# Three of layer 1's six modulation groups move from layer 0's choice of tokens to layer 1's output stage

## The reference, cut to what matters

```
sh1, sc1, g1, sh2, sc2, g2 = split((silu(c) @ ada_w + ada_b), 6)
csh1, csc1, cg1, csh2, csc2, cg2 = split(silu(c_ctx) @ ada_w + ada_b, 6)
hl = rmsnorm(xl, norm1_g) * (1 + sc1) + sh1
...
xl = xl + g1 * (concatenate([a_l, b_l, cv_l]) @ w_o)
xl = xl + g2 * ec_ffn(rmsnorm(xl, norm2_g) * (1 + sc2) + sh2, router_w, w_gate, w_up, w_down)
```

## Time and profile before

| | us |
|---|---|
| median of three runs | 4601.5 |
| lowest and highest | 4600.21 and 4602.4 |
| the profiled execution | 4604.36 |
| its span in the trace | 4602.6 |
| PE busy, of the span | 4057.6 (88%) |
| DVE busy | 2123.7 (46%) |
| ACT busy | 1224.3 (27%) |
| POOL busy | 731.9 (16%) |

### The profile page before, as it was taken

How to read it: one execution, slowest core, us unless ns; L and a number is a source line. 1 busy time by engine, 2 the same in 40 slices (tenths; PEclk the granted TensorE clock), 3 DMA queues, 4 the chain that set the end, 5 groups by cost and what they waited for, 6 DMA issues and landing times. The chain is left out here.

```text
span 4602.6 us, 76751 instructions
## 1 busy us (share of the span) xinstructions
PE 4057.6 (88%) x30527; PEld 2782.0 (60%) x30527; DVE 2123.7 (46%) x4242; ACT 1224.3 (27%) x2442; POOL 731.9 (16%) x858
## 2 busy tenths in 40 slices
PE   6998989987999799899986998999887988699994
PEld 4674557444888577566544886767566645465552
DVE  1213547226555422455425553121196767565554
ACT  1112336131000111244421000111165433133333
POOL 0110000311111011000111110000173042122222
PEclk8998999988999899999988999999899989799997
DMA  7115101348877611411129996311251312599995
GB/s 252 41 47 133 24 11 39 120 161 336 273 275 266 185 60 47 122 24 44 37 83 368 332 336 228 135 50 41 85 129 45 90 61 105 195 388 382 383 383 229
DMA packets 234733, 752.83 MB, mean 164 GB/s; under 512 B 62884, under 2 KB 139244, under 8 KB 216872
## 3 DMA queue, kind: packets, MB, share of 16 engines
q1 hardware_dynamic: 206664, 647.49, 39.5%
q0 software_dynamic: 21808, 73.42, 5.9%
q10 hardware_dynamic: 6000, 28.31, 1.6%
HBM read 650.48 MB, written 107.06 MB: 165 GB/s over the span
## 5 line engine op out<-in xcount | busy, mean ns | idle before, releaser
L3611 PE MATMUL bexp_gu<-up,bexp_xT 128*32 128x256 f32 x6144 | 342.0, 382 | 32.2 <-DMA up<-in_w_expert_up 18.2
L3611 PEld LDWEIGHTS bexp_gu<-up,bexp_xT 128*32 128x32 f32 x6144 | 209.1, 111 | 163.9 <-issue 33.2
L2059 PE MATMUL l0exp_gu<-l0exp_xT,l0e_held 128*128 128x160 f32 x2048 | 288.2, 302 | 4.5 <-DVE l0exp_xT L2103 4.5
L2059 PEld LDWEIGHTS l0exp_gu<-l0exp_xT,l0e_held 128*128 128x128 f32 x2048 | 280.7, 191 | 11.4 <-issue 6.2
L2059 PEld LDWEIGHTS l1exp_gu<-l1exp_xT,l1e_held 128*128 128x128 f32 x2048 | 233.8, 193 | 10.3 <-issue 7.2
L2059 PE MATMUL l1exp_gu<-l1exp_xT,l1e_held 128*128 128x128 f32 x2048 | 235.4, 276 | 2.7 <-DVE l1exp_xT L2103 2.7
L627 PE MATMUL p_ring<-p_hT,p_wc 128*128 128x256 f32 x1008 | 220.7, 382 | 4.8 <-DMA p_wc<-in_w_in 4.8
L3562 ACT ACTIVATE bexp_y<-bexp_acc,slot_gates 32x256 f32<-32x256 f32 x384 | 179.1, 467 | 148.2 <-PE bexp_acc L3596 139.2
L627 PEld LDWEIGHTS p_ring<-p_hT,p_wc 128*128 128x128 f32 x1008 | 192.5, 191 | 31.6 <-issue 5.1
L635 PE MATMUL p_ring<-p_wt,p_hT 128*128 128x400 f32 (+2 forms) x480 | 170.8, 516 | 0.0
L1119 PE MATMUL l0mla_scores<-l0mla_kT,l0mla_qT 96*128 96x512 f32 (+1 forms) x312 | 143.0, 546 | 21.1 <-DMA l0mla_qT<-RT 15.3
(11 more groups left out here) (700 smaller groups left out, 7756.9 us busy)
## 6 DMA issues: line engine op xcount, KB each, us to landing
up<-in_w_expert_up SPq DMA_DIRECT2D x31, 4096.0 KB, 23.8
l0e_held<-in_exp_w_gate SPq DMA_DIRECT2D x16, 2048.0 KB, 8.1
l0e_held<-in_exp_w_up SPq DMA_DIRECT2D x16, 2048.0 KB, 13.2
l0e_held<-in_exp_w_down SPq DMA_DIRECT2D x16, 2048.0 KB, 12.0
l1e_held<-in_exp_w_gate SPq DMA_DIRECT2D x16, 2048.0 KB, 8.4
l1e_held<-in_exp_w_up SPq DMA_DIRECT2D x16, 2048.0 KB, 12.9
l1e_held<-in_exp_w_down SPq DMA_DIRECT2D x16, 2048.0 KB, 13.3
near_space<-in_w_expert_down SPq DMA_DIRECT2D x16, 2048.0 KB, 24.3
```

The source lines that it names most:

```text
L2059: mm = nc.tensor.matmul(gu[g % 2][:, h, :], w[j][:, k, f * 128:(f + 1) * 128], xT[j][:, k, :], start=(k == 0), stop=(k == KD - 1))
L3611: mm = nc.tensor.matmul(gu[r][32 * c:32 * c + 32, 0:2 * HN].rearrange("p (h n) -> p h n", h=2), xT[j][:, k, 32 * r:32 * r + 32], both[:, : ...
```

## The change

Layer 0's choice of tokens makes groups 0 to 2 of layer 1. Layer 1's output stage makes groups 3 to 5, as layer 0's does for its own layer. Layer 1's choice still makes all six groups of the second block.

```
@@ -2185,7 +2185,7 @@
                             conv=(P1, Z, t["conv_w"][l], lambda tile: 1 if tile < CTX_TILES else 3),
-                            modulate=(lambda st: modulate(st, 0, [3, 4, 5], 1)) if l == 0 else None, energy=energy)
+                            modulate=lambda st: modulate(st, l, [3, 4, 5], 1), energy=energy)
@@ -2196,7 +2196,7 @@
                 route_choice(nc, n + "route", choices, X, a2, b2, t["router_w"][l], XN, energy, identity,
-                             lambda st: modulate(st, l + 1, list(range(6)), 3, expert.held), expert)
+                             lambda st: modulate(st, l + 1, list(range(3 if both else 6)), 3, expert.held), expert)
```

## The result

| | median us | runs | lowest and highest |
|---|---|---|---|
| before | 4602.4 | 9 | 4598.28 and 4613.57 |
| changed | 4618.5 | 9 | 4610.90 and 4628.58 |

The ratio is 1.0029, with a 95% interval of 1.0020 to 1.0037: 9 to 17 us slower, by the medians 16.1. The forecast was 4618.8 and +17.3. In a later series the changed kernel stood at 1.0027 (1.0017 to 1.0037). The profiled execution has a span of 4618.8 us, 16.2 over that of before.

The account below looks back on a forecast made before the run. It took DVE's search to bound layer 0's choice and PE layer 1's output stage. Blocks 16.72, clock 1.79, opening -1.21 and 0 elsewhere gave +17.3 us, a median of 4618.8 us, range 4614 to 4625.

Parts of the forecast that it names:

- The search sets layer 0's choice: Layer 0's choice of tokens: DVE's 36.84 us search sets the time, so removing groups 3 to 5 gains 0.
- about 27 us: Layer 0's choice: PE's idle time before the final transposes would grow from 7 to this, with DVE as releaser.
- 19.70 us: Layer 0's choice: how much earlier PE would be done without groups 3 to 5, 1068.99 in place of 1088.69.
- the rival of the time given back: Layer 0's choice: PE's chain of groups, not the search, releases the final transposes; sum -2.4 us, 4599.1 us; chance 4%.
- 1.43 us: End of layer 0's choice: possible gain from the barrier holding POOL, as the last gate store goes; kept as other end.
- The first expert's earlier loads: Layer 0's choice: SP issues the loads behind products 0 and 1, nobody waits for them; 0 both ways.
- The blocks: Layer 1's output stage: three added groups between tiles cost 6.61, 6.45 and 3.66 us, together 16.72 us.
- The clock: Behind the groups in layer 1's output stage: one fall of 1.69 us plus 0.10, 1.79 us; ends 0 and 5.07.
- The opening: Start of layer 1's output stage to its third tile: 1.21 us shorter with the load, as in layer 0.
- The end "+1": Opening of layer 1's output stage: other end, +1 us, with first convolutions late and the clock no better.
- The sum: Whole kernel: 16.72 + 1.79 - 1.21 + 0 = +17.3 us, median 4618.8 us, 0.38% slower.

Follow-up runs that it names:

- the removed half alone: Against the kernel before, layer 0's choice makes groups 0 to 2 only; nobody makes 3 to 5, layer 0's stand in: 0.9998, -1 us.
- e1: Against the kernel before, layer 0's choice keeps six groups and layer 1's output stage makes groups 3 to 5 once more: 1.0040, +18 us.
- e4: Against the kernel before, layer 1's choice makes both gates last and issues the first expert's loads ahead of the late stores: 0.9996, -2 us.
- e0: The changed kernel once more, against the kernel before: 1.0027, +12 us.
- e6: Kernel before with gates last in both choices, layer 0's choice products behind the last transpose of shares, late output-stage transposes in layer 0: 0.9992, -4 us.
- e10: Kernel with gates last and late transposes, one second-block gate moved from layer 1's choice to its output stage: 0.9977, -11 us against the kernel before.

## Why the prediction was right

- *The search sets layer 0's choice, and the removed groups are worth 0.* Shown: the removed half alone moved nothing (-6 to +3 us), PE's idle time grew to 32 us with DVE as its releaser, and the search kept its 36.8 us. The "about 27 us" of the forecast was a wrong reading, and with it the 19.70 us: PE was said to be done at 1068.99, but that is the end of group 3, one of those that leave. The last group that stays is group 2, in the order of time of the kernel before (a window of its own):

```profile
1057.33 6.23 PE L161 MATMUL l0route_modacc<-l0e_held,silu 128*2 128x256 f32 x64
```

It ends at 1063.56, 25.13 us ahead of 1088.69, and 25.13 + 6.97 is 32.10. The step was priced at 0, so the forecast did not suffer, but the rival of the time given back would have been worth 25.1 us and not 19.7. The prediction also overlooked that POOL's last row ended only 0.11 us before DVE's next step; where the two meet (e1, e4), the six groups cost up to 1.5 us, a gain for which it had no term (its 1.43 us were those of the barrier).

- *The first expert's earlier loads change nothing.* From the final transposes to the first expert transpose it is 7.29 us (before 7.22), and from there to the end of layer 0's experts as long as before.
- *The blocks.* 8.55, 8.38 and 5.38 us were forecast from layer 0 at 8.55, 8.39 and 5.38. The sum of 16.72 stands.
- *The clock.* One fall of 1.69 us and the 0.10 were taken, and that is what the profile has. That there was exactly one is in part luck. The reason for it, "once in two", was too coarse: in the old form of the block, in seven profiles of layer 0's stage and four of layer 1's, the records behind the first group were slow in 9 of 11, and those behind the second in 2 of 11. That is 11 falls in 11 stages, one for each on the average, as taken; single stages had none, one or two. The Trainium skill (TensorE: Matmul & The Clock Gate, "What's actually happening") says that activity releases the half rate. With the transposes late, the same two-row products stood alone between the tiles, with no idle time behind them, and in 16 blocks of eight stages the clock never fell behind them. So the traces fit the rule only through what else the old block had, the 1.70 us of waiting and the eight small transposes behind it. The edit moved both at once, and which of them it was no run shows.
- *The opening.* The step was right in its sign and too small: -1.21 was taken, -2.07 came. The 34.80 repeats (34.85, 34.87 and 34.81 in three others with three groups and the first 48 products at full clock; 35.91 with the gate 5 alone), and without a load it is 36.3 to 36.9. Layer 0, from which the term was taken, has 34.8 to 35.9. The end "+1" was not wide enough: where the first 48 products took 22.56 us in place of 20.87, four stages with and without a load took 38.7 to 39.1 us.
- *The sum.* The stage grew by 16.53 where 17.3 was forecast, the difference being the opening. The span's 16.2 is close to this in part by luck, as said above. The median moved by 16.1; the ratio's interval, 9 to 17 us, holds the 16.1 and ends just below 17.3, and in the series of e0 it is 8 to 17 us around 12.
- *The rivals.* The one on the other side (the chain releases the lists) did not happen in layer 0. It came true there where the search ended 5.6 us earlier and the chain 9.1 us later (e6), and in layer 1's choice, which the prediction did not look at, it was true already in the kernel before (8.01 us of DVE's waiting).

## What to carry to other kernels

Ask of each piece of work whether it stands beside the step that sets the stage or ahead of it: the same products were worth nothing behind the last transpose of shares and 5.7 us ahead of it. Ask also what a move does to the loads that wait for it: with six groups the same move stopped the weights and lost 6 us. Free time on an engine is worth using up to the point at which both chains end together, and not by halves. Where a stage already does elsewhere what a change adds here, its rows price the added blocks to the tenth of a microsecond; the clock and the start of the stage moved the sum by 2 to 4 us from profile to profile. A wait inside such a block (1.70 us, and the clock behind it) is worth moving a tile away.

## What the runs showed of the hardware that I had not expected

- Behind two-row products, a wait of 1.70 us and eight small transposes PE's clock fell to half for the next 3 to 4 us in 11 of 22 blocks (granted 0.59 and 0.55 in the windows above), and behind the products alone in none of 16. A fall costs about as much (1.69 us) as the wait itself.
- DVE's first merge step takes 0.28 us, and 1.98 or 1.99 in every profile in which POOL was adding a gate's row of 2 x 1024 at that moment (layer 1's choice in all but e10, layer 0's in e6). In layer 1's choice of the kernel before:

```profile
2482.61 1.98 DVE L1935 TENSOR_TENSOR l1route_ahead<-l1route_chosen,l1route_other 16x128 f32<-16x128 f32 x1 [8.01 <-ACT l1route_other_f L1771]
```

```profile
2482.12 2.33 POOL L200 TENSOR_TENSOR l1route_modrow<-l1route_modrow,l1route_modbias_row 2x1024 f32<-2x1024 f32 x1 [6.58 <-ACT l1route_modrow L173]
```

DVE's step ends at 2484.59, right behind POOL's at 2484.45. With one group fewer (e10) the two were apart, and it took 0.28. The step ahead of the merge, which turns uint32 into f32, met such a row in e1: its first record took 1.71 us, in the kernel before 0.21. The search's steps were not slowed by such a row in either layer (MAX8 0.69 us throughout). Why the row holds up some steps and not others was not tested.
